# A mixture-of-experts transformer block and a two-layer hybrid block in one kernel: the router by token halves, the branch around the overflow rounds ahead of the last expert sum, the rotary step without TensorE

## Chip, cores and metric

The kernel runs on one core of a Trainium2 chip, in one launch. The metric is the device time of that launch in microseconds (us). PE is TensorE (matrix products; PEld is its weight load), DVE is VectorE, ACT is ScalarE, POOL is GpSimd, and SP is the engine whose queue issues most of the DMAs.

## The reference, cut to what matters

256 tokens of width 1024 go through a first block (three mixers, a layer norm, a mixture of experts, a layer norm) and then through two layers of a second block. Of the first block the part that the change touches is the routing:

```
g_logits = x @ w_rg + b_rg                    # 4 groups
grp = argmax(g_logits);  p_grp = softmax(g_logits)[grp]
e_logits = (x @ w_re[g] + b_re[g]) for g = grp   # 8 experts of that group
top_val, top_idx = top_k(e_logits, 2)
gate = softmax(top_val) * p_grp
out[token] = sum over its 2 experts of gate * ((silu(x @ w_gate[e]) * (x @ w_up[e])) @ w_down[e])
x = layer_norm(ALPHA * x + out)
```

Of the second block:

```
proj = rms_norm(x) @ w_in                 # 24 tiles of 128 columns
dq, dk = apply_rope(...), gq, gk = apply_axial_rope(rms_norm(...))   # x1*cos - x2*sin, x2*cos + x1*sin
three kinds of attention (differential, grouped, memory), each gated by silu
x = x + rms_norm(concat @ w_out)
```

## The kernel before, in words

Everything is float32. Large products are made of three products of float32r halves: `product` (L851 to L853) multiplies high by high, low by high and high by low. ACT makes the high part of each weight tile (`high`, L1572), DVE subtracts it for the low part (`low`, L2187), each about three tiles ahead of PE. `AT_EXPERTS` are the first three tiles of the second block, whose halves are made at the end of the experts.

A list of turns, `TURNS`, fixes the order. Each turn holds jobs and possibly an attention step. A job is one product of PE into bank 6 or 7 in turn, and one copy out of it ("take") by ACT or DVE (`TAKEN_BY_DVE`); job j may start when job j - 2 has been taken. All engines walk through the same list.

The router comes behind the last output product `y1`. DVE normalises the tokens 0 to 127, then 128 to 255 (`moments`, `centred`, `scaled`; ACT makes the inverse root in `layer_stats`). Then four jobs `x1t` turn x (16 transposes), `logit` makes the 36 logits for all 256 tokens, with the 36 router columns as weights, `logitT` turns them back to token order, `route` on DVE picks the group, the two experts and their gates in a chain in which each operation waits for the one before (`link`), and `rank` counts with five products of PE how many earlier tokens chose the same expert.

The 32 experts are worked on in eight bunches of four, each expert with 32 places for tokens. Per bunch DVE writes a matrix of places (`places`) and its product with the gates, PE gathers the tokens through the first (`gather_half`, twice), makes gate and up products (`gate_up`, L1247), turns the hidden values, makes the down products (`down`, L1261) and adds them back through the weighed places (`add_back`, L1233) into four banks of PSUM that collect the sum for all tokens. Overflow rounds for experts with more than 32 tokens stand in a branch on every engine behind the last sum; for these inputs it is not entered. Four products with zeros close the sum (L1352). Expert weights stream in through 21 slots in the order of use. `load_expert` lets SP wait until a slot is free: for the first items of bunch 0 that is `gu_half`, the end of the first half of its gate and up products.

In each layer of the second block ten tiles get the rotary step. PE multiplies the tile by a permutation (`swap`, L1031), so that each row gets its partner 16 rows away, DVE multiplies this with the sines (L1879), the tile with the cosines (L1880), and adds (L1883). Six of the ten stand in the opening of a layer, one behind each of the tiles 1 to 5 and the last after the first scores; the four others (tiles 12 to 15, with a norm factor of `hsq`) in the attention steps.

## Time and profile before

| | us |
|---|---|
| median of 3 runs (lowest, highest) | 754.43 (753.81, 759.05) |
| the profiled execution | 761.98 |
| its span, first to last instruction | 760.2 |
| busy in the span: PE, DVE, ACT, POOL | 682.1, 368.4, 324.3, 16.8 |

The mean granted clock of PE is 0.952 of full speed. Shares of busy time are means over stages that have different limits; the chain that ended last tells which engine was waited for, and windows and the timeline tell it for one stage.

### The profile page before, as it was taken

What the parts mean: (1) busy time and instruction counts of PE and PEld (TensorE: products, weight loads), DVE (VectorE), ACT (ScalarE), POOL (GpSimd) and SP (SyncE); (2) the same over time, 40 slices, a digit from 0 to 9 for tenths busy, and PEclk for the clock granted to TensorE, in tenths of its full rate; (3) what the DMA queues carried; (4) which work ended last, traced back from release to release, by engine and by line L of the source; (5) the groups of instructions that cost most, each with busy time, mean ns of one, the idle gap of its engine ahead of it and who ended that gap; (6) DMA issues with size and microseconds to landing.
All of it is one profiled execution on the core that took longest, in us unless ns stands there. A gap on an engine that the chain in (4) does not pass through costs nothing.

```text
span 760.2 us, 11653 instructions
## 1 busy us (share of the span) xinstructions
PE 682.1 (90%) x4580; PEld 520.5 (68%) x4582; DVE 368.4 (48%) x813; ACT 324.3 (43%) x759; POOL 16.8 (2%) x31
## 2 busy tenths in 40 slices
PE   6989999996599999798796799999979999999986
PEld 4968998695343455264251388878859898888876
DVE  1633657445432132021121456678775466787733
ACT  2565665421000112020120243678865545788742
POOL 5001000000000000000000000000000000000000
PEclk9999999898589999898989899999999999999999
DMA  9967331399959999999999729008163080073301
GB/s 280 340 201 246 111 112 56 123 302 367 315 223 350 414 410 414 415 409 416 414 410 411 251 88 300 1 1 274 61 221 111 1 274 5 1 231 103 111 1 56
DMA packets 94616, 167.80 MB, mean 221 GB/s; under 512 B 4238, under 2 KB 75648, under 8 KB 90464
## 3 DMA queue, kind: packets, MB, share of 16 engines
q1 hardware_dynamic: 92272, 160.88, 59.0%
q0 software_dynamic: 2160, 6.07, 2.3%
q8 instruction: 39, 0.64, 0.3%
q14 instruction: 17, 0.14, 0.1%
q10 hardware_dynamic: 128, 0.08, 0.0%
HBM read 165.93 MB, written 1.07 MB: 220 GB/s over the span
## 4 chain that ended last, share of the span: by engine, by line
PE 72%; SPq 11%; DMA 5%; ACT 5%; DVE 4%; issue 2%; ACTq 0%; DVEq 0%
PE psum L851 13%; PE psum L853 11%; PE psum L852 11%; SPq L741 9%; PE psum L1206 4%; PE psum L1247 4%; PE psum L894 4%; PE psum L1145 3%; DMA ring<-in_w_expert_down_dram 3%; PE psum L1261 3%; PE psum L1192 2%; DMA ring<-in_w_expert_up_dram 2%; PE psum L986 2%; PE psum L1104 2%; PE psum L1233 1%
## 5 line engine op out<-in xcount | busy, mean ns | idle before, releaser
L851 PE MATMUL psum<-a_high,w_high 128*128 128x256 f32 x512 | 150.9, 295 | 2.1 <-ACT q_c L1472 1.3
L853 PE MATMUL psum<-a_high,w_low 128*128 128x256 f32 x512 | 144.7, 283 | 0.0
L852 PE MATMUL psum<-x_low,w_high 128*128 128x256 f32 x512 | 144.6, 283 | 0.0
L2187 DVE TENSOR_TENSOR w_low<-ring,w_high 128x1024 fp32r<-128x1024 f32 (+1 forms) x79 | 111.2, 1421 | 23.4 <-ACT w_high L1572 23.3
L851 PEld LDWEIGHTS psum<-a_high,w_high 128*128 128x128 f32 x512 | 97.7, 191 | 13.8 <-issue 4.7
L1572 ACT ACTIVATE w_high<-ring 128x1024 fp32r<-128x1024 f32 (+1 forms) x79 | 95.9, 1219 | 9.6 <-DMA ring<-in_w_in_dram 6.2
L852 PEld LDWEIGHTS psum<-x_low,w_high 128*128 128x128 f32 x512 | 97.8, 191 | 0.4
L853 PEld LDWEIGHTS psum<-a_high,w_low 128*128 128x128 f32 x512 | 97.8, 191 | 0.0
L851 PE MATMUL psum<-w_high,a_high 128*128 128x256 f32 x240 | 69.6, 290 | 0.0
L852 PE MATMUL psum<-w_low,a_high 128*128 128x256 f32 x240 | 68.5, 285 | 0.0
L1247 PE MATMUL psum<-ring,q_c 128*32 128x512 f32 x320 | 55.1, 682 | 11.0 <-DMA ring<-in_w_expert_up_dram 7.0
L1206 PEld LDWEIGHTS psum<-tiles,x_nat 128*128 128x128 f32 x256 | 55.2, 307 | 9.1 <-issue 9.1
L1206 PE MATMUL psum<-tiles,x_nat 128*128 128x128 f32 x256 | 56.9, 382 | 2.1 <-DVE tiles L2104 2.1
L853 PE MATMUL psum<-w_high,mix_low 128*128 128x256 f32 x192 | 54.8, 286 | 0.0
L2115 DVE TENSOR_SCALAR tiles<-tiles 128x256 f32<-128x256 f32 x8 | 2.3, 292 | 101.2 <-ACT tiles L1620 101.2
L851 PEld LDWEIGHTS psum<-w_high,a_high 128*128 128x128 f32 x240 | 46.7, 195 | 3.2 <-issue 2.3
L852 PEld LDWEIGHTS psum<-w_low,a_high 128*128 128x128 f32 x240 | 46.8, 195 | 0.0
L1620 ACT ACTIVATE tiles<-psum 128x256 f32<-128x256 f32 x8 | 3.1, 383 | 97.1 <-PE psum L1247 97.1
L1247 PEld LDWEIGHTS psum<-ring,q_c 128*32 128x32 f32 x320 | 13.6, 123 | 42.5 <-issue 42.5
L853 PEld LDWEIGHTS psum<-w_high,mix_low 128*128 128x128 f32 x192 | 37.4, 195 | 0.0
L1614 ACT ACTIVATE q_c<-psum 128x512 f32<-128x512 f32 x16 | 9.6, 597 | 62.7 <-PE psum L1206 62.7
L1145 PE MATMUL psum<-const,probs 128*128 128x128 f32 x200 | 32.2, 283 | 4.5 <-DVE probs L1973 2.4
(334 smaller groups left out, 1190.4 us busy)
## 6 DMA issues: line engine op xcount, KB each, us to landing
ring<-in_w_in_dram SPq DMA_DIRECT2D x36, 1024.0 KB, 8.7
ring<-in_w_expert_down_dram SPq DMA_DIRECT2D x24, 1024.0 KB, 18.0
ring<-in_w_expert_gate_dram SPq DMA_DIRECT2D x40, 512.0 KB, 14.6
ring<-in_w_expert_up_dram SPq DMA_DIRECT2D x40, 512.0 KB, 15.3
ring<-in_w_out_dram SPq DMA_DIRECT2D x12, 1024.0 KB, 5.1
ring<-in_w_mem_kv_dram SPq DMA_DIRECT2D x4, 1024.0 KB, 16.5
k_c<-in_w_expert_gate_dram SPq DMA_DIRECT2D x5, 512.0 KB, 14.9
k_c<-in_w_expert_up_dram SPq DMA_DIRECT2D x5, 512.0 KB, 15.9
```

What stands on the lines that cost most here:

```text
L741: sp.dma_start(to[:, SLOT // 2 * m:SLOT // 2 * m + SLOT // 2].rearrange("p (k n) -> p k n", n=DE), w[:, 4 * half:4 * half + 4, :]).then_in ...
L851: pe.matmul(dst, left[0], right[0], start=first, stop=False)
L852: pe.matmul(dst, left[0], right[1], start=False, stop=False)
L853: return pe.matmul(dst, left[1], right[0], start=False, stop=last)
L894: mm = pe.matmul(dst, src[:, k, P * tt:P * tt + P], w[:, k, a:b], start=(k == 0), stop=(k == KC - 1))
L986: mm = pe.matmul(dst[:, 0:T], w[:, k, P * n:P * n + P], memT[l][:, k, :], start=(k == 0), stop=(k == KC - 1))
L1145: mm = pe.transpose(dst[:, P * c:P * c + P], pr[:, a:a + P], ident)
L1206: mm = pe.matmul(dst[:, P * c:P * c + P], x[:, k, :], places2[:, tt, :], start=(tt == 0), stop=(tt == 1))
L1247: mm = pe.matmul(bank(6)[PLACES * e:PLACES * e + PLACES, :], gathered2[b % 2][:, k, PLACES * e:PLACES * e + PLACES], w, start=(k == 0), st ...
L1261: mm = pe.matmul(bank((7, 5)[half])[PLACES * e:PLACES * e + PLACES, :], hiddenT[:, k, PLACES * e:PLACES * e + PLACES], expert_slot(n)[:, a ...
L1572: act.activation(split_like_raw(n)[0], raw_of(n), ACT.Copy).then_inc(highs, 1)
L2187: dve.tensor_tensor(w_l, raw_of(n), as_f32(w_h), ALU.subtract).then_inc(lows, 1)
```

## The change

- Router: `x1t` and `logit` are made per 128 tokens. The tokens are the weights now and the 36 router columns stream, so the logits come out in token order and `logitT` goes. The search for a first maximum merges comparison and multiplication. The mask of closed groups is added in one step. `rank` signals after three of its five products, the other two go to bank 3. The places of bunch 0 are compared at once (`locate_first`), the gates are made later (`gates_of`), and the first half of the gather waits for the places only.
- Experts: ACT makes the sigmoid of the gate (Exp, Ln, Exp), in place of an addition and a reciprocal of DVE. The branch stands on PE, ACT and DVE ahead of the last copies and the last sum, and the last sum closes the accumulation, so the products with zeros go. Overflow rounds each make the sum of the bunch before them.
- The first three low parts of the second block are made by GpSimd. ACT makes the third high part a little later.
- Rotary step: DVE shuffles the rows (`stream_shuffle`), GpSimd multiplies by the cosines into one of two buffers, and the swap jobs go from PE's list.

```diff
+PARTNER = [(m + 16) % 32 for m in range(32)]
-TAKEN_BY_DVE = ("bias", "xt2", "y1", "logit", "logitT", "rank", "swap")
+TAKEN_BY_DVE = ("bias", "xt2", "y1", "logit", "rank")
...
-    jobs += [("x1t", k) for k in range(4)] + [("logit",), ("logitT",), ("rank",)]
+    for tt in range(2):
+        jobs += [("x1t", tt, 0), ("x1t", tt, 1), ("logit", tt)]
+    jobs += [("rank",)]
...
 @@ GpSimd
+            for n in AT_EXPERTS:
+                pool.wait_ge(highs, n + 1)
+                w_h, w_l = split_like_raw(n)
+                pool.tensor_tensor(w_l, raw_of(n), as_f32(w_h), ALU.subtract).then_inc(lows, 1)
             pool.wait_ge(p_ready, JOB[("mv", 0, 1)] + 1)
             for n in range(LAYERS):
                 pool.dma_start(post_row[:, n, :], ...
+            for n, (l, t) in enumerate(ROPES):
+                pool.wait_ge(p_act, taken(JOB[("tile2", l, t)]))
+                if n >= 2:
+                    pool.wait_ge(roped, n - 1)
+                pool.tensor_tensor(cosined[n % 2], tile3[:, t, :], c_("cos_lin" if t < 6 else "cos_ax"), ALU.mult
+                                   ).then_inc(cosine, 1)
 @@ PE
                 elif kind == "x1t":
-                    pe.wait_ge(ln_done, 2)
-                    mm = turn4(dst, x4, job[1])
+                    tt, half = job[1:]
+                    pe.wait_ge(ln_done, tt + 1)
+                    for c in range(4):
+                        mm = pe.transpose(dst[:, P * c:P * c + P], x4[:, tt, 4 * half + c, :], ident)
                 elif kind == "logit":
-                    from_act(("x1t", 3))
+                    tt = job[1]
                     for k in range(KC):
-                        mm = pe.matmul(dst[0:GROUPS + EXPERTS, 0:T], router[:, k, :], xT3[:, k, :],
+                        if k % 4 == 0:
+                            from_act(("x1t", tt, k // 4))
+                        mm = pe.matmul(dst[:, 0:GROUPS + EXPERTS], xT3[:, k, P * tt:P * tt + P], router[:, k, :],
...
-                elif kind == "swap":
-                    l, n = job[1:]
-                    from_act(("tile2", l, n))
-                    mm = pe.matmul(dst[:, 0:T], swap, tile3[:, n, :], start=True, stop=True)
...
-                pe.wait_ge(p_dve, taken(JOB[("rank",)]))
                 pe.wait_ge(setup, 2)
-                pe.wait_ge(placed, 1)
+                pe.wait_ge(located, 1)
                 gather_half(0, 0)
+                pe.wait_ge(p_dve, taken(JOB[("rank",)]))
...
-                    pe.wait_ge(y0_out, b + 1)
-                    pe.wait_ge(y1_out, b + 1)
-                    add_back(backs[b % 2])
+                    if b + 1 < BUNCHES:
+                        pe.wait_ge(y0_out, b + 1)
+                        pe.wait_ge(y1_out, b + 1)
+                        add_back(backs[b % 2])
                 pe.wait_ge(memT_out, KC // 2)
                 with pe.If(some):
...
-                for b in range(4):
-                    mm = pe.matmul(bank(b), zeros_b[:, 0:P], zeros_b[:, :], start=False, stop=True, skip_group_check=True)
-                    if b % 2 == 1:
-                        mm.then_inc(moe_done, 1)
+                pe.wait_ge(y0_out, BUNCHES)
+                pe.wait_ge(y1_out, BUNCHES)
+                add_back(backs[1], last=True)
 @@ ACT
-            def gate_exp(i):
+            def gate_exp(i, then):
                 act.wait_ge(gu_ready, i + 1)
-                act.activation(gate_e, bank(6)[:, 0:DE], ACT.Exp, scale=-1.0).then_inc(gate_exped, 1)
+                then(act.activation(gate_e, bank(6)[:, 0:DE], ACT.Exp, scale=-1.0))
+                then(act.activation(gate_e, gate_e, ACT.Ln, bias=1.0))
+                act.activation(gate_e, gate_e, ACT.Exp, scale=-1.0).then_inc(gate_exped, 1)
...
+                y_due(BUNCHES - 1)
+                y_half()
                 act.wait_ge(y_ready, 2 * BUNCHES)
-                for n in AT_EXPERTS:
-                    high(n)
+                high(AT_EXPERTS[0])
                 layer_stats(1, 0)
+                high(AT_EXPERTS[1])
...
                     if job == ("mk", 0, 1):
+                        high(AT_EXPERTS[2])
                         layer_stats(1, 1)
 @@ DVE
+            def rope(l, n):
+                tl = tile3[:, n, :]
+                m = rope_nth(l, n)
+                if m > 1:
+                    dve.wait_ge(roped, m - 1)
+                dve.wait_ge(p_act, taken(JOB[("tile2", l, n)]))
+                link(dve.stream_shuffle(rope_a, tl, PARTNER))
+                op = dve.tensor_tensor(rope_a, rope_a, c_("sin_lin" if n < 6 else "sin_ax"), ALU.mult)
+                dve.wait_ge(cosine, m)
+                link(op)
+                op = dve.tensor_tensor(tl, cosined[(m - 1) % 2], rope_a, ALU.add)
+                if n >= 12:
+                    dve.wait_ge(p_act, taken(JOB[("hsq", l, n)]))
+                    link(op)
+                    op = dve.tensor_tensor(tl, tl, sq_tile(n), ALU.mult)
+                op.then_inc(roped, 1)
...
-                link(dve.tensor_tensor(score3, values3, wide(best), ALU.is_equal))
-                link(dve.tensor_tensor(score3, score3, order, ALU.mult))
+                for tt in range(2):
+                    op = dve.scalar_tensor_tensor(score3[:, tt], values3[:, tt], best[:, tt:tt + 1], order,
+                                                  ALU.is_equal, ALU.mult)
+                link(op)
...
+            def locate_first(src):
+                dve.wait_ge(ranked, 1)
+                link(dve.tensor_tensor(rank, src[:, 0:2 * EXPERTS], e_sc, ALU.add))
+                for tt in range(2):
+                    op = located_in(0, None, tt)
+                op.then_inc(located, 1)
...
-                then(dve.tensor_scalar(gate_e, gate_e, 1.0, None, ALU.add))
-                then(dve.reciprocal(gate_e, gate_e))
                 then(dve.tensor_tensor(gate_e, gate_e, bank(6)[:, 0:DE], ALU.mult))
...
             def experts():
-                places(0, None, link)
+                gates_of()
+                dve.wait_ge(located, 1)
+                weigh(0)
...
-                for n in AT_EXPERTS:
-                    low(n)
+                dve.wait_ge(y_ready, 2 * BUNCHES)
+                y_half()
                 dve.wait_ge(moe_done, 1)
```

## Rows read from the trace of the kernel before

**Rows 1.** The page, its part 4: the chain that ended last.

```profile
PE 72%; SPq 11%; DMA 5%; ACT 5%; DVE 4%; issue 2%; ACTq 0%; DVEq 0%
```

**Rows 2.** Windows of 1 us: busy times, then PE's clock, DMA share, GB/s.

```profile
182.00:183.00 1.00, 0.00 (x0) 0.00 (x0) 0.96 (x2) 0.00 (x0) 0.00 (x0) 0.80 1.10 375
196.00:197.00 1.00, 0.00 (x0) 0.00 (x0) 0.90 (x7) 0.21 (x1) 0.00 (x0) 0.63 1.10 346
206.00:207.00 1.00, 1.00 (x6) 1.00 (x6) 0.00 (x0) 0.00 (x0) 0.00 (x0) 0.50 0.58 229
208.00:209.00 1.00, 0.70 (x4) 0.41 (x2) 0.00 (x0) 0.26 (x1) 0.00 (x0) 0.50 0.00 0
216.00:217.00 1.00, 1.00 (x11) 0.92 (x9) 0.00 (x0) 0.02 (x1) 0.16 (x1) 1.00 0.59 131
```

**Rows 3.** Timeline of the router: start, duration, engine, operation, idle before and releaser.

```profile
181.09 0.20 ACT L1548 ACTIVATE small<-small 128x1 f32<-128x1 f32 x1
182.29 1.28 DVE L2011 SCALAR_TENSOR_TENSOR x_nat<-x_nat,small,tiles 128x1024 f32<-128x1024 f32 x1
183.73 3.75 PE L901 MATMUL psum<-const,x_nat 128*128 128x128 f32 x16 [5.01 <-DVE x_nat L2011]
184.85 0.60 ACT L1413 ACTIVATE xT<-psum 128x512 f32<-128x512 f32 x1 [3.56 <-PE psum L901]
188.21 5.91 PE L998 MATMUL psum<-xT,router_w 128*36 128x256 f32 x16 [0.73 <-ACT xT L1413]
195.09 0.23 DVE L1855 COPY probs<-psum 128x72 f32<-128x72 f32 x1 [0.47 <-PE psum L1004]
200.16 0.22 DVE L2049 TENSOR_TENSOR probs<-probs 128x64 f32<-128x64 f32 x1
200.53 0.60 PE L1010 MATMUL psum<-probs,const 128*128 128x32 f32 x2 [5.47 <-DVE probs L2049]
201.37 0.61 PE L1012 MATMUL psum<-probs 128*128 128x32 f32 x2
202.94 0.22 DVE L1864 TENSOR_TENSOR probs<-psum,probs 128x64 f32<-128x64 f32 x1 [0.62 <-PE psum L1014]
203.80 0.48 DVE L2100 TENSOR_TENSOR tiles<-probs,const 128x128 f32<-128x128 f32 x2
204.95 3.75 PE L1206 MATMUL psum<-tiles,x_nat 128*128 128x128 f32 x16 [2.12 <-DVE tiles L2104]
```

**Rows 4.** Timeline of the end of the experts.

```profile
418.45 5.15 PE L1261 MATMUL psum<-ring,tiles 128*32 128x512 f32 x32 [0.95 <-DMA ring<-in_w_expert_down_dram]
423.66 0.69 DVE L2123 COPY values<-psum 128x512 f32<-128x512 f32 x1 [6.73 <-PE psum L1261]
424.50 3.67 PE L1233 MATMUL psum<-values,tiles 128*128 128x512 f32 x8 [0.90 <-DVE values L2123]
431.37 1.07 PE L1352 MATMUL psum<-zeros_b 128*128 128x512 bf16 x3 [3.20 <-issue]
```

**Rows 5.** Timeline of the opening of the second block's first layer.

```profile
455.81 0.39 ACT L1463 ACTIVATE tiles<-psum 128x256 f32<-128x256 f32 x1 [1.54 <-PE psum L853]
458.69 0.38 ACT L1463 ACTIVATE tiles<-psum 128x256 f32<-128x256 f32 x1 [1.55 <-PE psum L853]
459.12 0.19 PEld L851 LDWEIGHTS psum<-a_high,w_high 128*128 128x128 f32 x1 [0.44 <-ACT tiles L1463]
462.29 0.38 ACT L1463 ACTIVATE tiles<-psum 128x256 f32<-128x256 f32 x1 [2.28 <-PE psum L853]
472.91 0.60 PE L1031 MATMUL psum<-tiles,const 128*128 128x256 f32 x2
457.17 1.22 DVE L2187 TENSOR_TENSOR w_low<-ring,w_high 128x1024 fp32r<-128x1024 f32 x1 [1.64 <-ACT w_high L1572]
459.58 0.43 DVE L1880 TENSOR_TENSOR tiles<-tiles,const 128x256 f32<-128x256 f32 x1
```

**Rows 6.** A window of 50 us in the steps: columns as in rows 2, PE first.

```profile
480.00:530.00 50.00, 47.87 (x362) 41.43 (x361) 37.86 (x84) 37.15 (x102) 0.00 (x0) 1.00 0.28 89
```

More of the change, by code:

```diff
@@ L241 @@
 TURNS = schedule()
-JOBS = [job for jobs, _ in TURNS for job in jobs]
+JOBS = [job for jobs, _ in TURNS for job in jobs if job[0] != "swap"]
+ROPES = [job[1:] for jobs, _ in TURNS for job in jobs if job[0] == "swap"]
 JOB = {job: n for n, job in enumerate(JOBS)}
@@ L558, in build @@
         rope_a = q_c[:, 7 * T:8 * T]
+        cosined = [router_w[:, 0:T], c_("places")]
         def sq_tile(n):
@@ L634, in build @@
         act_chain, dve_chain, moe_chain = sem("act_chain"), sem("dve_chain"), sem("moe_chain")
+        more_act_chain = sem("more_act_chain")
         stored = sem("stored")
         def rope_nth(l, n):
-            order = [j[2] for j in JOBS if j[0] == "swap" and j[1] == l]
-            return l * len(order) + order.index(n) + 1
+            return ROPES.index((l, n)) + 1
         def silu_nth(l, n):
@@ L1227, in turn_hidden, with add_back @@
                 mm.then_inc(hT_ready, 1)
-            def add_back(back):
+            def add_back(back, last=False):
                 for tt in range(2):
@@ L1233, in add_back @@
                         mm = pe.matmul(bank(2 * tt + half), back[:, P * tt:P * tt + P],
-                                       y_e[:, 512 * half:512 * half + 512], start=False, stop=False,
+                                       y_e[:, 512 * half:512 * half + 512], start=False, stop=last,
                                        skip_group_check=True)
-                mm.then_inc(summed, 1)
+                    if last:
+                        mm.then_inc(moe_done, 1)
+                if not last:
+                    mm.then_inc(summed, 1)
             def gate_up(b, half):
@@ L1364, in _ @@
                 for job in jobs:
+                    if job[0] == "swap":
+                        continue
                     run(job, j)
@@ L1409, in take @@
                     op = act.activation(vecs[:, :], src[:, 0:41], ACT.Copy)
-                elif kind in ("xt", "x1t"):
+                elif kind == "xt":
                     k = job[1]
-                    to = xT_1 if kind == "xt" else xT3
-                    op = act.activation(to[:, 2 * k:2 * k + 2, :], src.rearrange("p (c t) -> p c t", c=2), ACT.Copy)
+                    op = act.activation(xT_1[:, 2 * k:2 * k + 2, :], src.rearrange("p (c t) -> p c t", c=2), ACT.Copy)
+                elif kind == "x1t":
+                    tt, half = job[1:]
+                    op = act.activation(xT3[:, 4 * half:4 * half + 4, P * tt:P * tt + P],
+                                        src.rearrange("p (c t) -> p c t", c=4), ACT.Copy)
                 elif kind == "cnat":
@@ L1681, in _ @@
                 for job in jobs:
+                    if job[0] == "swap":
+                        continue
                     for n in SPLIT_AT.get(j, ()):
@@ L1712, in _ @@
                         layer_stats(0, job[2])
-                    elif job[0] == "logitT":
+                    elif job == ("logit", 1):
                         act.wait_ge(route_dif, 1)
@@ L2269, in _ @@
                 for job in jobs:
+                    if job[0] == "swap":
+                        rope(*job[1:])
+                        for n in lows_now:
+                            low(n)
+                        lows_now = []
+                        continue
                     if job == ("cnat", 0):
@@ L2285, in _ @@
                         lambda_sums()
+                    if job == ("rank",):
+                        locate_first(bank(6 + j % 2))
                     if BY_DVE[j]:
@@ L2297, in _ @@
                         scaled(0, job[2])
-                    if job == ("logitT",):
-                        route()
+                    if job == ("x1t", 0, 0):
+                        dve.memset(ones, 1.0)
+                    if job == ("logit", 1):
+                        choose()
                     if job[0] == "tile2" and job[2] in GATE_TILES:
```

174 lines of the change are left out of this document (86 added, 88 removed).

## The prediction

> **What bounds the kernel now.** I read the page first, then the chain of waits, then windows of one and fifty microseconds, then the timeline of three places. The chain [rows 1] is PE for 72% and the DMA queue of SP for 11%, nearly all of it with the expert weights. So there are three regimes. Before 178 us and after 444 us PE is the bound: 47.87 us busy in the 50 us of [rows 6]. Between, the expert weights are streamed, and the DMA sets the pace. In front of the stream lies the router, a serial stretch in which all engines wait for one another: DMA still works off what was queued, falls silent at 206.6 us, and moves nothing until 216.4 [rows 2], because every slot is full and the first is given back only when the first half of bunch 0's gate and up products is done. Until then 1 us at the router is 1 us of the whole: the stream is full again afterwards and its end at 418.45, where PE waits for the last down weights [rows 4], moves with its start.
>
> **Part 1, the router (removed: one logit job, its copies, some links of DVE's chain; moved: work of the first 128 tokens ahead).** Before [rows 3]: the second half of the layer norm ends at 183.57 (182.29 + 1.28), 16 transposes take 3.75, eight logit products with 256 columns 5.91, and the logits lie in token order at 195.32 (195.09 + 0.23).
> After the change, with PE at its low clock as before: ACT is free at 181.3 (it serves the second variance first, 181.09 + 0.20), copies the first tokens' two halves by 182.5 (0.60 each), and PE makes their eight logit products from 181.95. They load 128x128 weights and stream 36 columns; the nearest rows are the rank products, 0.42 apart at the low clock (two from 200.53, the third from 201.37), so eight take 3.5 at the low clock. Some of them fall before the clock drops, which was at 182.6 [rows 2]: end about 185. Then four transposes (0.94), a copy (0.60), four more transposes and their copy beside the first four products, and the last four products: 185.9, 186.5, about 188.5, 190.3; DVE's addition 0.25. Logits at 190.5 instead of 195.32: -4.8.
> DVE's choice took 5.06 from there to 200.38 (200.16 + 0.22). The change merges two linked operations in each of three searches and drops one link and the multiplication from the mask: a link costs about 0.25 at 64 columns, an unlinked neighbour 0.1. I count 0.13 + 0.38 + 0.21 + 0.22: -0.95.
> Rank: PE's fifth product had to end before DVE began at 202.94; now three are enough (two products of 0.43 less), and between them and the first gather stand one addition (0.26, a 64-column operation with its link) and the two comparisons (0.48) in place of four small operations, these two, and the two that weigh: the gather's start was 2.01 after 202.94, now it is 0.9. Together -2.0. The gate weights and the weighing (nine links, about 2.3) move behind; they are needed only after the second half of the gather, 10 us later, where PE's first half gather and first products cover them. If that cover were gone they would cost 2.3.
> Sum -7.8, taken as **-8**. Bounds: if the clock stays high through logits and rank, the three PE pieces halve and the gather starts 11.9 earlier (logits at 187.2, rank 1.3 shorter at half price); if ACT's copies and the smaller matmuls gain only half of what I say, 5. I take the low clock, since it fell at 182.6 and again at 196.6 with PE as little used as it will be. Is the 8 passed on? The stream was silent for 9.8 us; 8 of them vanish, the last item queued still lands at 206.6, and the first slot comes free at about 207. So yes, all of it, and a gain over about 10 would begin to meet data that is not there.
>
> **Part 2, the end of the experts (moved: the branch ahead of the last sum; removed: the four closing products).** In [rows 4] the last down product of PE begins its run at 418.45 and DVE copies its half from 423.66 to 424.35; the last sum runs 424.50 to 428.17; then PE issues nothing for 3.20 us, the branch; the closing products take 1.07, to 432.44. After: branch from 423.66 to 426.9, the copies beside it, sum 3.67 to 430.5, and nothing more. The first tokens' sum is complete at 428.7 instead of 431.9, but PE's next product starts at 430.5 instead of 432.4: **-1.9**. The following stretch is PE's (memory keys and values), with DVE's layer norm beside it, which gains 3.2 and so stays ahead. DVE and ACT take the branch too, now ahead of the last copies. Both reach it when the last hidden products are turned, before the down products begin at 418.45, and their copies are wanted by 426.9: with 3.2 for each that fits. If theirs took 4 us longer than PE's they would begin to show. Bounds: -3.2 if the layer norm were what ends last, 0 if branch and copies run one after another.
> The gate's reciprocal (ACT now makes the sigmoid by Ln and Exp) shortens DVE's chain before the hidden products by about 1 us per bunch. Nothing is paid for it: behind the first seven stands a gather, behind the last the down weights' arrival [rows 4].
> Low parts of the next layer's first three tiles: DVE 1.22 each [rows 5], on GpSimd not shown in this trace. GpSimd starts them when ACT's high parts are there, at about 428, and PE wants the first at 450. Even 5 us each would fit. What is queued behind them on GpSimd is the load of the post-norm rows, wanted at the end of the layer. 0, but see the third rival.
>
> **Part 3, the rotary step (removed: 20 PE products; added: 20 DVE shuffles, 20 GpSimd products).** A swap product is two records, 0.60 in its row at 472.91, of which the next product overlaps a little: 0.53. Its price is higher in the opening of a layer [rows 5]: the next tile's weight load at 459.12 waited 0.44 for ACT's copy of the tile before, because with the swap in between the tile needs that one's bank. Copies of tiles come 3.60 apart with a swap (458.69 to 462.29), and 2.88 without (455.81 to 458.69). So 0.72 for four swaps a layer. The other two of the opening I take at 0.53, the four in the steps at 0.45, where PE is 96% busy [rows 6] and ACT's exponentials sometimes end last. 2.88 + 1.06 + 1.8 = 5.7 a layer, **-11.5** for both. Bounds: -14.4 if all cost 0.72; -8 if only the opening returns it and the steps do not, with a little lost to DVE.
> On DVE three operations of 0.43 stay three: shuffle, product, sum. The shuffle is in no row; the nearest is the product of the same size, 0.43; bounds 0.2 and 0.9. GpSimd's product of 128x256 is in no row either; nearest again 0.43 on DVE, bounds 0.4 and 3. It starts at ACT's copy, a tile earlier than DVE's rotary step, so even 2.8 would be hidden behind one tile. DVE waits for it, and the low parts of later tiles are queued behind this wait; they are three tiles ahead of PE. Per tile DVE works 1.22 + 1.3 = 2.5 of the 2.88 that are left: the cover becomes thin.
> The Trainium skill ("SBUF — State Buffer", "Who interferes with whom") speaks against this: a DVE instruction with two SBUF inputs contends with a GpSimd instruction that reads SBUF, and one blocks fully. No run here shows it so far. "GPSIMD Engine Reference", section 3.1, has GpSimd's tensor_tensor at 1.96 times DVE's time; by that its product would take about 0.85 (an estimate from the page and 0.43), and the sum would be the same.
>
> **The sum.** 8 + 1.9 + 11.5 = 21.4. The profiled execution took 761.98 us (span 760.2), so 740.6 of its kind; the median of the runs shown is 754.43, 7.5 below, and I take the same 21.4 off: **733.0**. The parts lie behind one another and do not share an engine's time, so they add.
>
> **Rivals.** (a) The router's gain is larger: clock high, 11.9 instead of 8, and perhaps the first gather at half its 3.75 [rows 3] and a like part of the products behind it: 725 to 729. For: PE's pause is 2.3 us now, from 179.7 to 181.95, instead of 5.3. Against: the clock fell at 196.6 though the logit products had run to 194.1 [rows 3].
> (b) The router's gain does not reach the end, since DMA is what ends last: 741. Against it stand the zeros in [rows 2]. It holds only if transfers that start 8 earlier meet something else busy; nothing is.
> (c) DVE becomes the bound of the openings: if each GpSimd product of some 0.9 blocks DVE, its 2.5 per tile becomes 3.4, 0.5 above 2.88, over ten tiles with some lead; the opening then returns about half, and the steps, with DVE 76% busy, lose some too: 6 of 11.5 lost, 739. By the skill's rule this is what would happen; the kernel's rows only leave it room.
> (d) Slower than before: GpSimd's product is so slow that the first scores of each layer wait for the rotary step. They need the fourth tile's, so four products in sequence against 14.4 us of PE's tiles. Each layer loses 4g - 14.4, and the whole 21.4 is eaten at g = 6.3 us, fifteen times DVE's 0.43; at 7 us it gives 760.
> (e) The branch shows on ACT or DVE and part 2 becomes a loss of some us: 736 to 738.
>
> **Chances.** Forecast (sum within 4 us) 0.50; (a) 0.17; (b) 0.07; (c) 0.15; (d) 0.03; (e) 0.08. Eight in ten: 724 to 743. Within 1% (about what a measurement of this kernel can tell from no change) is 747 to 762: reached if (b) and (c) meet, 0.07; slower is (d), 0.03; faster 0.90.
>
> **What the changed profile would show.** The first gather at about 197 instead of 204.95; DMA's gap at 207 to 208.4 instead of 9.8 us; logits in two groups of eight products. The last down product at about 410.5; then 3.2 us of issue ahead of the last sum, and the first memory product 12 us after the start of the last down products instead of 14. Tile copies 2.88 apart in both openings; no line of swaps. GpSimd products under 1 us, and DVE's low parts still 1.22; if they stretch, (c) is at work. What would make it wrong: a clock that behaves differently in the router, a DVE chain slower than its count of links, and GpSimd.

## The result: a third of the forecast gain

The changed kernel took 751.51 us (median of 8 runs, 744.20 to 752.28), the kernel before, on the same chips, 758.52 (8 runs, 753.81 to 763.87). The ratio is 0.989, 95% interval 0.986 to 0.992: 8.3 us faster by the ratio, 7.0 by the medians, where 21.4 were forecast, and outside the forecast's range. Of the 18.5 us between 733.0 and 751.51, 4.1 are the starting point (three runs of before had their median at 754.43, the eight at 758.52); the other 14.4 are gain that did not come.

The profiled execution of the changed kernel took 747.01 us (span 745.2), 15.0 less than that of before. This pair flatters the change: the one lies 4.5 below the median of its kernel, the other 3.5 above.

**The router after.** Timeline; the first row stands against the first of [rows 3], the second variance.

```profile
178.34 0.20 ACT L1571 ACTIVATE small<-small 128x1 f32<-128x1 f32 x1
179.17 2.22 PE L1020 MATMUL psum<-router_w,xT 128*128 128x36 f32 x16 [2.05 <-ACT xT L1435]
183.07 3.60 PE L1020 MATMUL psum<-router_w,xT 128*128 128x36 f32 x16
186.71 0.19 DVE L1897 TENSOR_TENSOR probs<-psum,small 128x36 f32<-128x36 f32 x1 [5.09 <-PE psum L1020]
191.15 0.22 DVE L2085 TENSOR_TENSOR probs<-probs 128x64 f32<-128x64 f32 x1
193.08 0.23 DVE L2093 TENSOR_TENSOR probs<-psum,probs 128x64 f32<-128x64 f32 x1 [1.48 <-PE psum L1028]
193.34 0.50 DVE L2146 TENSOR_TENSOR tiles<-probs,const 128x128 f32<-128x128 f32 x2
193.99 3.75 PE L1218 MATMUL psum<-tiles,x_nat 128*128 128x128 f32 x16 [0.15 <-DVE tiles L2146]
```

From variance to first gather: 204.95 - 181.09 = 23.86 before, 193.99 - 178.34 = 15.65 after, so -8.2. Its pieces: variance to logits 14.23 before and 8.56 after (-5.7); the choice 5.06 and 4.47 (-0.6); choice to gather 4.57 and 2.62 (-1.95). The two groups of logits show the clock: the same 16 records take 2.22 us where it was full until 180.7, and 3.60 after it fell. The other 2.75 us by which the gather is early (204.95 - 193.99 = 10.96 in all) were there before the router began.

**The end of the experts after**, against [rows 4]; and the DMA queues in the silence, as the stretch in which PE issues nothing is called from here on.

```profile
406.92 6.54 PE L1276 MATMUL psum<-ring,tiles 128*32 128x512 f32 x32 [0.86 <-DMA ring<-in_w_expert_down_dram]
413.52 0.69 DVE L2178 COPY values<-psum 128x512 f32<-128x512 f32 x1 [8.02 <-PE psum L1276]
414.95 2.81 PE L1245 MATMUL psum<-values,tiles 128*128 128x512 f32 x6 [1.50 <-DVE values L2178]
420.92 1.02 PE L1245 MATMUL psum<-values,tiles 128*128 128x512 f32 x2 [3.16 <-issue]
421.78 2.54 PE L1004 MATMUL psum<-bias,ring 128*128 128x256 f32 x11
```

```profile
q1 hardware_dynamic: 567, 0.56, 46.3%
q8 instruction: 1, 0.02, 1.9%
```

From the end of the last down product to the next layer's first product it is 8.32 us (413.46 to 421.78) and was 8.64 (423.60 to 432.24): -0.3 instead of -1.9. The silence stayed, and it was not the branch alone: it now stands in the middle of the last sum, behind the branch by 2.8 us of products. The queue rows (columns: packets, MB, share; window 417.5 to 421.2) show what happens in it: one packet of 16 KB on q8, a queue of kind "instruction". In the kernel before one packet of this queue falls into the silence too, between 428.2 and 428.9, and none between 418.5 and 428.1. The profiles do not name the engine that a queue serves, but there are fourteen silences of 2.0 us or more in the eighteen profiles of this document, and each ends 2.4 to 2.8 us after such a packet started, wherever it stands (here 418.48 and 420.92, before 428.54 and 431.37). So I read it as PE waiting for its own code. It does not need full queues: the queues' share is 0.99 in before's silence and falls to 0.27 in this one. The Trainium skill ("Runtime: NRT & Kernel Launch", "Instruction fetch mechanics") says that code comes in 16 KiB blocks, that crossing into the next is mostly hidden, and that a taken branch to code outside the blocks at hand breaks the fetching ahead. The 16 KB packet agrees with the first and the silence of 3.16 us not with the second; on the third see e6 and e15.

**The layers after.** Timeline: layer norm and GpSimd, then copies of tiles (against [rows 5]); then groups of instructions, with busy us and mean ns.

```profile
423.51 1.23 DVE L2048 SCALAR_TENSOR_TENSOR x_nat<-x_nat,small,tiles 128x1024 f32<-128x1024 f32 x1
426.84 2.35 POOL L848 TENSOR_TENSOR w_low<-ring,w_high 128x1024 fp32r<-128x1024 f32 x1 [4.42 <-ACT w_high L1595]
427.28 2.98 DVE L2048 SCALAR_TENSOR_TENSOR x_nat<-x_nat,small,tiles 128x1024 f32<-128x1024 f32 x1 [1.22 <-ACT small L1571]
452.52 0.39 ACT L1486 ACTIVATE tiles<-psum 128x256 f32<-128x256 f32 x1 [1.55 <-PE psum L871]
455.40 0.39 ACT L1486 ACTIVATE tiles<-psum 128x256 f32<-128x256 f32 x1 [1.46 <-PE psum L871]
```

```profile
L858 POOL TENSOR_TENSOR router_w<-tiles,const 128x256 f32<-128x256 f32 x10 | 9.3, 926 | 149.8 <-ACT tiles L1486 109.7 <-ACT tiles L1481 40.1
L858 POOL TENSOR_TENSOR const<-tiles,const 128x256 f32<-128x256 f32 x10 | 7.9, 787 | 40.7 <-ACT tiles L1481 29.0 <-ACT tiles L1486 11.7
L1916 DVE TENSOR_TENSOR q_c<-q_c,const 128x256 f32<-128x256 f32 x20 | 9.1, 454 | 0.7
L1915 DVE STREAM_SHUFFLE q_c<-tiles 128x256 f32<-128x256 f32 x20 | 9.0, 448 | 0.1
```

Tiles are copied 2.88 us apart, GpSimd's products take 0.93 and 0.79 us, the shuffle 0.45: all three as forecast. GpSimd does hold VectorE up where both read long operands (2.98 instead of 1.23 us: VectorE's scaling begins 0.44 after GpSimd's subtraction and ends 1.07 after it), but in a place with slack. By that, the trace agrees with the rule of the Trainium skill that the forecast cited ("SBUF — State Buffer", "Who interferes with whom"). What the forecast did not see is this: the timeline ahead of the second G step of the second layer (a G step is one of the grouped attention), and two windows with the columns of [rows 2]. Then the same place in the kernel before.

```profile
660.35 0.43 DVE L2269 TENSOR_TENSOR tiles<-tiles,k_c 128x256 f32<-128x256 f32 x1 [0.67 <-ACT k_c L1508]
661.46 0.44 DVE L1915 STREAM_SHUFFLE q_c<-tiles 128x256 f32<-128x256 f32 x1
662.99 0.42 DVE L1923 TENSOR_TENSOR tiles<-tiles,q_c 128x256 f32<-128x256 f32 x1
663.33 2.35 DVE L2251 TENSOR_TENSOR w_low<-ring,w_high 128x1024 fp32r<-128x1024 f32 x2
664.69 0.36 PE L869 MATMUL psum<-a_high,w_high 128*128 128x256 f32 x1 [2.00 <-DVE w_low L2251]
```

```profile
661.00:665.00 4.00, 2.00 (x15) 1.68 (x15) 3.65 (x8) 3.97 (x12) 0.00 (x0) 1.00 0.52 165
665.00:669.00 4.00, 4.00 (x23) 4.00 (x22) 3.83 (x10) 2.56 (x8) 0.00 (x0) 0.57 0.52 165
```

```profile
677.14 0.42 DVE L2205 TENSOR_TENSOR tiles<-tiles,k_c 128x256 f32<-128x256 f32 x1
679.95 1.22 DVE L2187 TENSOR_TENSOR w_low<-ring,w_high 128x1024 fp32r<-128x1024 f32 x1
681.32 0.36 PE L851 MATMUL psum<-a_high,w_high 128*128 128x256 f32 x1 [0.65 <-ACT q_c L1472]
```

PE waits 2.0 us for a low part that VectorE makes behind the gates and behind the rotary sums, and then works at a mean clock of 0.57. The step from one G score to the next took 10.80 us before (675.16 to 685.96) and takes 13.22 here (657.61 to 670.83); in the first layer 10.79 and 11.73. The wait is 2.0 us in both layers; the difference between them is the clock, which fell only behind the second (in e4's profile it fell behind both, and both steps take 13.2).

The order of VectorE's work at this place is that of the kernel before: gates, rotary operations, low parts. But there it had hardly any slack. Counted from the scores, the first low part began at 4.79 us and was ready at about 6.0, and the product that needs it ran at 6.16. Now it begins at 5.72, since the first gate waits for ScalarE (it begins at 2.74 instead of 1.98) and the four rotary operations take 0.16 longer, while PE, without the swap product, stands ready at 5.08 instead of 5.51.

### The profile page after: what moved, and what is told of

Read it like the earlier page. It is cut to its first block, busy times and chain, and to the rows that moved or that the text cites. A ratio compares the mean times of both kernels' runs of the same rounds, so it can differ in the third digit from the quotient of the medians.

```text
span 745.2 us, 11661 instructions
## 1 busy us (share of the span) xinstructions
PE 666.1 (89%) x4551; PEld 515.1 (69%) x4552; DVE 351.3 (47%) x810; ACT 330.4 (44%) x775; POOL 41.1 (6%) x54
## 3 DMA queue, kind: packets, MB, share of 16 engines
HBM read 165.95 MB, written 1.07 MB: 224 GB/s over the span
## 4 chain that ended last, share of the span: by engine, by line
PE 60%; SPq 13%; DMA 9%; DVE 8%; ACT 6%; issue 3%; DVEq 0%; ACTq 0%
SPq L746 11%; PE psum L869 11%; PE psum L871 10%; PE psum L870 10%; PE psum L1218 3%; PE psum L1262 3%; DMA ring<-in_w_expert_down_dram 3%; DMA ring<-in_w_in_dram 2%; PE psum L1157 2%; PE psum L1276 2%; DMA ring<-in_w_expert_up_dram 2%; PE psum L912 2%; PE psum L1004 2%; SPq L749 2%; PE psum L1204 2%
## 5 line engine op out<-in xcount | busy, mean ns | idle before, releaser
L2251 DVE TENSOR_TENSOR w_low<-ring,w_high 128x1024 fp32r<-128x1024 f32 (+1 forms) x76 | 107.8, 1430 | 16.1 <-ACT w_high L1595 16.1
L2173 DVE TENSOR_TENSOR tiles<-tiles,psum 128x256 f32<-128x256 f32 x8 | 3.4, 422 | 110.1 <-ACT tiles L1645 110.1
L1245 PE MATMUL psum<-values,tiles 128*128 128x512 f32 x64 | 29.5, 601 | 8.6 <-DVE values L2178 5.5
```

What stands on the lines that cost most here:

```text
L1245: mm = pe.matmul(bank(2 * tt + half), back[:, P * tt:P * tt + P], y_e[:, 512 * half:512 * half + 512], start=False, stop=last, skip_group_ ...
L2251: dve.tensor_tensor(w_l, raw_of(n), as_f32(w_h), ALU.subtract).then_inc(lows, 1)
```

## The experiments

All ratios are to the kernel before on the same chip, with 95% intervals; medians are in us. The changed kernel itself stands at 0.989.

**The parts one by one.** Three kernels make each one part of the change in the kernel before: e1 the router, e2 the rotary step, e3 the end of the experts (sum, branch, sigmoid) with the three low parts on GpSimd. The fourth is the changed kernel with satisfied waits at the head of PE's code:

```
+            for _ in range(40):
+                pe.wait_ge(const_in, 16)
```

> The kernel before with the router's part alone. The forecast's term was 8 us. If the router is worth what the changed profile shows (first gather 8.2 us earlier against the last output product, end of the expert stream 7.4 earlier), this is 8 us below the kernel before, ratio 0.989 to 0.990, and nearly the whole gain of the change. Rival: the two profiles differ by run-to-run luck of PE's clock and the part is worth 4 us or less, ratio 0.995 or above.

> The kernel before with the rotary part alone (no swap products, shuffle on DVE, cosines on GpSimd). The forecast's term was 11.5 us, ratio 0.985. Theory now: only the openings return it (some 3.3 us a layer) and the steps are held by the chain of scores, maximum, exponentials, high part and low part, so that later PE pauses longer and part is given back: 4 to 5 us, ratio 0.994. Rival: nothing at all, the openings' gain is fully given back in the steps, ratio 0.998 to 1.002.

> The kernel before with the end of the experts alone (branch ahead of the last sum, no closing products, sigmoid on ACT, three low parts on GpSimd). The forecast's term was 1.9 us, ratio 0.9975. Theory now: the 3.2 us of silence belong to the fetch of the next block of instructions, not to the branch, and stay on the path wherever a block ends; 0 to 2 us, depending on where this kernel's blocks end. In its profile the silence stands either at the branch or inside the last sum. Rival: the silence is the branch's own cost and stands ahead of the last sum, and the kernel gains 1.9.

> The changed kernel with 40 satisfied waits at the head of PE's program, done while PE waits for the first transfer, so that everything behind lies 40 instructions later in the stream. If the 3.16 us of silence inside the last sum is a fetch at the end of a block of instructions, it moves away from the middle of the sum: either to the branch (then up to 1.5 us are gained) or off the path (3 us). If it belongs to the branch or to a wait, it stays between the third and the fourth product of the last sum, and the time is that of the changed kernel, ratio 0.989.

Measured: e1 753.34, ratio 0.9945 (0.992 to 0.997), 4.2 us faster; e2 753.85, 0.9925 (0.989 to 0.996), 5.7 us; e3 757.88, 1.0003 (0.997 to 1.003), nothing. Their sum, 9.7, agrees with the whole, 8.3, each part being known to 2 or 3 us either way. e4: 748.33, 0.986 (0.982 to 0.991). In e4 the silence has moved, by 40 instructions that do no work, from the seventh record of the sum to the first; with PE's unshifted code it stands at the seventh record in all three profiles that there are (the changed kernel, e5, e14). In e3 it stands ahead of the sum too. The rows are e3's, then e4's:

```profile
427.08 5.37 PE L1237 MATMUL psum<-values,tiles 128*128 128x512 f32 x8 [3.48 <-issue]
```

```profile
415.94 5.37 PE L1248 MATMUL psum<-values,tiles 128*128 128x512 f32 x8 [3.41 <-issue]
```

In both rows the sum also takes 5.37 us instead of 3.67: the clock fell in it (mean 0.67 and 0.68). So a silence there costs 1.7 us more than its own length; e10's, of 3.33 us, did not (3.67 at full clock).

**The pause in the G steps.** e5 and e14 (one kernel, run twice) take the low parts straight after the row maxima:

```
                     maxes(step)
+                    for n in lows_due:
+                        low(n)
...
-                    if not jobs or jobs[0][0] != "swap":
-                        for n in lows_now:
-                            low(n)
```

> The changed kernel with one edit: in every attention step VectorE takes the low part of the next weight slice straight after the step's row maxima, ahead of the gates and ahead of the rotary sums, which the change had put first. Theory (the pause of TensorE at the second G step, 2.2 us in the second layer and some 0.9 us in the first, is VectorE's low part coming late behind the moved rotary work): both pauses shrink to the 0.6 us that the kernel before shows, and the drop of the clock behind the second one goes too; 2.5 to 4 us faster than the changed kernel, ratio to the kernel before 0.984 to 0.986. Rival (the chain scores, row maxima, exponentials, turned product sets these steps, and the rotary sums are now what is late): no gain, 0.989, or a loss of 1 to 2 us.

> The kernel of the low parts taken early, once more. Theory of the layout: 0.982 to 0.986 again, with a silence of about 3 us or two of them between the last down product and the next layer. Rival (luck): 0.976 to 0.980, as the padded ones.

Measured: 745.76, 0.984 (0.980 to 0.989), and 746.70, 0.984 (0.981 to 0.988). In e5's profile the pause is gone in both layers (G step 10.59 us twice), and the clock behind it stays up:

```profile
660.23 2.35 DVE L2251 TENSOR_TENSOR w_low<-ring,w_high 128x1024 fp32r<-128x1024 f32 x2
662.50 0.75 DVE L2269 TENSOR_TENSOR tiles<-tiles,k_c 128x256 f32<-128x256 f32 x2
663.18 0.43 DVE L1915 STREAM_SHUFFLE q_c<-tiles 128x256 f32<-128x256 f32 x1
```

```profile
665.00:669.00 4.00, 4.00 (x34) 3.17 (x34) 3.83 (x11) 3.75 (x11) 0.00 (x0) 1.00 0.50 170
```

Little became late instead (first to last D score, those of the differential attention: 37.37 us, 37.12 in the changed kernel). By ratios and medians, these late low parts cost the changed kernel some 4 to 6 us; each interval by itself meets that of the changed kernel, and the two runs taken together differ from it by a little over two standard errors.

**The branch.** e6 is the changed kernel, e15 that of the low parts, both without the overflow rounds on any engine (these inputs need none, but a kernel without them computes only such inputs).

> The changed kernel without the overflow rounds on every engine: no flag is loaded and no branch is taken at the end of the experts (with these inputs no round is needed, the output is that of the reference). Theory (the silence of 3.2 us at the end of the experts is TensorE's sequencer fetching a block of code that the jump over the rounds kept from being fetched ahead, and the branch itself costs another 0.6 to 0.7 us now that it stands ahead of the last sum): from the last down product to the first product of the next layer 4.6 to 5.2 us instead of 8.3, so 3 to 4 us faster than the changed kernel, ratio 0.984 to 0.985. Rival (a block of code is fetched late there in any layout, because the queues are full of weights): the silence stays at 3.2 us, at another instruction, ratio 0.988 to 0.989.

> Low parts early and no overflow rounds on any engine (none is needed with these inputs). If the two effects are separate they add: 3 us less than without the branch alone, 5 us less than the low parts alone, ratio 0.974 to 0.977, and 4.4 us from the last down product to the next layer. Rival (both had removed the same pause, or their runs were lucky): 0.979 to 0.981.

Measured: e6 743.92, 0.979 (0.974 to 0.984); e15 741.33, 0.976 (0.972 to 0.980). From the last down product to the next layer it is 4.4 us in both, with no silence (of the sixteen profiles with the branch, thirteen have one). The rows are e6's:

```profile
418.43 3.67 PE L1226 MATMUL psum<-values,tiles 128*128 128x512 f32 x8 [0.90 <-DVE values L2142]
421.94 1.24 PE L985 MATMUL psum<-bias,ring 128*128 128x256 f32 x5
```

PE's price of branch and fetch is thus 3.9 us between these two profiles, as expected. The medians gained more, 7.6 against the changed kernel and 5.4 against e14, and e6's ratio lies below the range expected for it; whether the surplus is chance or the branch of another engine was not tried.

**Only the place of the code.** Satisfied waits inside the overflow rounds, which are never entered: 100 of them (e9) and 180 (e10) in the kernel of the low parts, 100 in the changed kernel (e13).

```
                                 more_bunch(n)
+                                for _ in range(100):
+                                    pe.wait_ge(memT_out, KC // 2)
```

> The kernel of the low parts taken early, with 100 satisfied waits added to TensorE's code inside the overflow rounds, which are never entered with these inputs: nothing more is executed, only the code behind the branch lies further on. Theory (the silence is a fetch of code after the jump, and its place is that of a block's border): the 3.2 us move away from the seventh product of the last sum, to another instruction, or vanish where the border falls far enough behind the jump; 0 to 3.3 us faster than the kernel of the low parts alone, ratio 0.980 to 0.984. Rival (the silence belongs to those products, a semaphore or a port): it stays at the same instruction.

> The same with 180 waits in the rounds that aren't entered. Theory: another place again for the silence, and at most one of the two layouts has it before the first product of the sum, where it costs most (3.5 us); a layout without it ends the experts some 3.3 us sooner, ratio 0.980. Rival: as in the run before, no change of place.

> The changed kernel with 100 satisfied waits inside the overflow rounds, which are not entered, and nothing else. Theory (the layout of the code sets how often and where the fetch is exposed): 2 to 4 us faster than the changed kernel, ratio 0.984 to 0.986. Rival (the gain of the padded kernels over the low parts alone was luck of the executions): ratio 0.988 to 0.990.

Measured: e9 742.73, 0.976 (0.972 to 0.980); e10 741.99, 0.9765 (0.973 to 0.980); e13 747.07, 0.984 (0.980 to 0.989). Each median is 3.0 to 4.7 us below those of its kernel without the padding, though nothing more or less is executed. For e9 and e10 the intervals hardly touch those of e5 and e14; e13's meets that of the changed kernel. The profiles show part of it: e9 has almost no silence (PE is idle for 1.73 us ahead of the sum instead of 0.90), e10 has one of 3.33, e13 one of 2.37 and 1.6 us more inside the sum, by the clock (0.68). e14, without padding, has one of 2.20 and e5 two:

```profile
414.24 2.81 PE L1245 MATMUL psum<-values,tiles 128*128 128x512 f32 x6 [3.29 <-issue]
420.20 1.86 PE L1245 MATMUL psum<-values,tiles 128*128 128x512 f32 x2 [3.14 <-issue]
```

From the last down product to the next layer the three profiles without padding (the changed kernel, e5, e14) take 8.7 us in the mean and the four with it (e9, e10, e13, e16) 6.7. With 100 waits the packet of code starts 0.4 to 1.0 us before the last down product ends (e9, e13, e16), in e5 0.5 after it. That is 2.0 of the 3 to 4.7 us; the rest is not explained.

**The same kernels again.** e11 is the kernel before once more, e12 the router part once more, each one execution with its profile (754.93 and 757.57 us).

> The kernel before, once more, for a second profile. Theory (the profile on which the forecast rests shows the clock of the router and of the mixers at its worst): a profile with other stretches of low clock ahead of 215 us and the first gather 2 to 5 us sooner than 204.95. Rival (the low stretches of 141 to 149, 182 to 193 and 196 to 214 us belong to the kernel): the same stretches again, first gather at 204.9.

> The router part alone, once more, for a second profile. Theory: the first gather lies between 194.9 us, as in its first profile, and 198 us, with another pattern of low clock; the mean of its two profiles stands 5 to 8 us ahead of the mean of those of the kernel before. Rival (the pattern belongs to the kernel): first gather again at 194.9 us, and the router's gain at that point again 10 us, so that it is lost further on.

The first four rows are e11's; they answer to the logits and the first gather in [rows 3] and to the last two of [rows 4]. Then its windows.

```profile
185.21 3.62 PE L998 MATMUL psum<-xT,router_w 128*36 128x256 f32 x16 [0.73 <-ACT xT L1413]
199.68 3.75 PE L1206 MATMUL psum<-tiles,x_nat 128*128 128x128 f32 x16 [2.13 <-DVE tiles L2104]
419.21 3.67 PE L1233 MATMUL psum<-values,tiles 128*128 128x512 f32 x8 [0.90 <-DVE values L2123]
422.93 0.81 PE L1352 MATMUL psum<-zeros_b 128*128 128x512 bf16 x3
```

```profile
141.00:149.00 8.00, 7.69 (x46) 5.55 (x47) 4.62 (x14) 4.17 (x9) 0.00 (x0) 1.00 0.56 182
184.00:191.00 7.00, 4.37 (x22) 2.16 (x20) 1.54 (x8) 1.07 (x2) 0.00 (x0) 0.99 1.10 348
```

The windows of the first profile of before, for 141 to 149 and for the logits:

```profile
141.00:149.00 8.00, 7.86 (x28) 5.18 (x26) 4.43 (x13) 2.20 (x7) 0.00 (x0) 0.57 0.51 162
182.00:193.00 11.00, 8.54 (x28) 5.14 (x29) 1.54 (x2) 2.39 (x4) 0.00 (x0) 0.53 1.10 350
```

One kernel, two executions: the first gather at 204.95 and at 199.68, and at the end of the experts a silence of 3.20 us and none at all (here the packet of code came between 416.5 and 417.5, under the down products). What moved the gather is the clock: 27 us low in the router (182 to 193 and 196 to 213) against 20 (181 to 184 and 191 to 208), and 7 us low at 141 to 149 against none there. Only 2.5 of the 5.3 us lie in the router: its second variance stands at 181.09 and at 178.31, so from there to the gather it is 23.86 and 21.37, and the logits, 5.91 and 3.62 us, are nearly all of this difference. e12's gather stands at 197.34, with 24 us low. The means of two, 202.3 and 196.1, put the router's gain there at 6.2 us; by the first pair (204.95 and 194.95) it was 10.0. From variance to gather the router part takes 17.00 (e1) and 16.25 us (e12), so by this length its gain is 6.0.

**Products that keep the clock up.** e7 is the kernel before, e8 the changed one, with products of constants in PE's pauses of the router.

```
+            def fill(n):
+                for _ in range(n):
+                    pe.matmul(bank(3)[:, 0:T], ident, const[:, P:P + T], start=True, stop=True)
```

> The kernel before, with products of constants that nobody reads put into TensorE's pauses in the router stage (11 ahead of the first turned tile, 4 ahead of the logits, 12 ahead of the ranks, 4 ahead of the first gather), so that the clock stays up. Together with the next run it asks how much of the router's forecast gain was the clock of one profiled execution. Theory (the profile of before showed the router at its worst, low for 27 us, and most executions have less of that): the stage ends 4 to 6 us earlier in the profile than that of the kernel before, the median gains only 1 to 3 us, ratio 0.996 to 0.999. Rival (every execution has the low clock there, it is part of the kernel): the median gains what the profile gains, ratio 0.992 to 0.994.

> The changed kernel with the same filling products in the router stage (4 and 2 ahead of the two groups of logits, 10 ahead of the ranks). Theory: the second group of logits takes 2.0 instead of 3.6 us, ranks and turned tiles lose another 1 us; first gather 2 to 3 us earlier, and the whole 1 to 3 us faster than the changed kernel, ratio 0.985 to 0.988. The difference between this run and the one before is the router change without the clock: by the chain of work 4 to 5 us of router, 8.5 to 9.5 us in all. Rival (the stream of expert weights, not the first gather, sets the end of the experts): first gather earlier, the end of the last down product not, ratio 0.989.

Measured: e7 757.66, 0.999 (0.996 to 1.002); e8 747.35, 0.982 (0.976 to 0.987). e7's profile has its first gather 2.5 us earlier and the last down product's end 4.2 earlier than the first profile of before; the ratio of 12 runs is worth less than 1 us. That fits the theory that this first profile was a bad one, but the stage did not end the 4 to 6 us earlier that I expected. e8 is no clean trial: its first fill started only when PE's wait was over and delayed the logits by the 3.4 us that it took (the two groups then ran in 1.98 and 1.87 us, instead of 2.22 and 3.60), the gather came 2.5 us later than in the changed kernel, and still the median is lower. I can't explain that; its interval meets that of the changed kernel.

**GpSimd's three low parts.** e16 is e9 with these three taken back by VectorE.

> The padded kernel of the low parts taken early (ratio 0.976), with the next layer's first three low parts taken back by VectorE as in the kernel before. Forecast on record: 0 us for this part. Theory: within 1 us, 0.975 to 0.978, since the three low parts lie beside the layer norms on either engine. Rival (GpSimd's 2.35 us products hold VectorE up, whose scaling took 2.98 instead of 1.28 us beside one of them): 1.5 to 2 us faster, 0.974, with the last scaling of the layer norm at 1.3 us. Other rival (VectorE's three products of 1.22 us now stand ahead of its layer norm): 2 to 3.5 us slower, 0.979 to 0.981.

Measured: 744.85, 0.980 (0.976 to 0.984), e9 at 0.976 (0.972 to 0.980): not told apart. In its profile the layer norm's last scaling takes 1.28 us instead of 2.10 in e9, but the norm ends 14.1 us after the start of the sum instead of 12.0 (1.7 of it because e16's sum ran at a mean clock of 0.68 and took 5.37 us), and from the first memory product to the first scores it is 36.4 us with either. So the work lies under PE's, wherever it is done.

## Why the prediction was wrong

Right were: the direction; what the edits do in the router and in the openings; GpSimd under 1 us; the tile distance of 2.88; and no rival of the five took the place of the forecast. Wrong were three terms of the sum: in the first a price, in the second what the silence is, in the third a cover taken for granted.

**Part 1, "-8".** The edits return what was worked out: -8.2 between the same two operations of one pair of profiles. The mistake is in what stood under it, one execution of before. The step that failed is the price of the stage before: "eight logit products with 256 columns 5.91" is that of a low clock over most of them, and "PE at its low clock as before" was taken for a property of the kernel. In another execution of the same kernel they take 3.62, and the stage is 2.5 us shorter. So the term of 8 is 6.0 by two profiles each of before and of the part alone, and 4.2 by the ratio of e1, whose interval (2 to 6) just reaches 6.0. How far a run's clock and its time go together can be read from all runs: with the time at low clock in a run taken as 2 x (1 - mean granted clock) x span, 68 runs of before and 116 of the other kernels lie about lines with a slope of 0.25 us for each us at low clock; the runs of before span 45 to 81 us of it and 753 to 765 us of time. As a price of the clock it fails: e7 took 17 us of low clock away and was 0.5 us faster in the mean than before on its chip. "Is the 8 passed on?" was answered rightly: the last down run starts 11.5 us earlier (406.92 against 418.45) where the gather was 11.0 earlier. It then takes 6.54 us instead of 5.15, without a wait inside, at a mean clock of 0.55 instead of 0.70, so 10.1 us are left at its end.

**Part 2, "-1.9".** It came to 0.3 in the profile and to nothing in e3. Failed has the step "then PE issues nothing for 3.20 us, the branch". By all that the runs show it is a wait for code, which moves with the layout of the code, is there in some executions only, and was joined in this profile by 0.6 us ahead of the sum (PE idle for 1.50 us instead of 0.90; in e14, with the same code on PE, it is 0.90). In six profiles with the branch behind the sum the way from down product to next layer is 8.64, 8.70, 8.42, 8.42, 5.27 and 5.27 us (mean 7.5), in the ten with the branch ahead of it 8.32, 8.68, 8.62, 10.90, 8.65, 5.24, 6.84, 7.52, 6.77 and 7.21 (mean 7.9). The closing products' 1.07 us are eaten by this, and by the clock that fell in the sum in five of the ten.

**Part 3, "-11.5".** It was 5.7. The openings pay nearly as forecast, 3.3 us each: from the start of the second memory product to the first scores of the second layer 24.26 before (603.36 to 627.62) and 20.92 after (589.71 to 610.63), 3.94 forecast. "The four in the steps at 0.45" are 1.8 a layer in the sum and 0.8 in the trace (first to last D score: 37.91 before, 37.12 after). And 0.9 and 2.4 us are lost at one G step of each layer, 2.4 where the clock fell behind the wait. The step that failed here is the cover: the forecast saw that "the low parts of later tiles are queued behind this wait" on VectorE and dismissed it with "they are three tiles ahead of PE". At this step the low part was 0.2 us ahead of its product in the kernel before, and it now comes 0.9 us later, 0.8 of it by ScalarE, which the forecast did not look at. 2 x (3.3 + 0.8) - 0.9 - 2.4 = 4.9, against 5.7 by e2's ratio.

**The sum.** "So 740.6 of its kind; ... I take the same 21.4 off" carried the luck of one execution into the gain, and three runs' median into the start.

**What stays open.** Why the block of code is fetched early in one execution and late in another, what more than 2 us the padding gives, why the medians of the kernels without a branch gained more than PE's silence, and why ScalarE comes 0.8 us later in the G step. The best kernels that still hold the overflow rounds are e9 and e10, 0.976 of before, with medians 9 us below that of the changed kernel.

## What to carry to other kernels

A duration from one execution is a price at that execution's clock: before such a row carries a term of a sum, take a second profile, or price the stretch at both levels of the clock. When a job changes its engine or loses its place in a queue, read at every place where it is issued how long what stands behind it was ready before it was needed, not at the usual one: here one low part with 0.2 us of slack cost nearly as much as the whole part returned, and moving a few lines brought it back. A pause marked "issue" near a branch may be code on its way, and the DMA queues of that window tell; then take the branch out or cover it, since moving work around it moves the pause along.

## What the hardware showed

- A block of code that is not there costs PE 2.0 to 3.5 us; it does so in 13 of 18 profiles, in one of them twice. The silence ends 2.4 to 2.8 us after the block's packet started, with the queues full (before) or at a share falling to 0.27 (the changed kernel). Forty satisfied waits at the head of the program moved the place of the stall by six records.
- The same code has another clock in another execution: the stretch of low clock at 141 to 149 us stands whole in six of the 18 profiles, half in three, not at all in nine, and the kernel before is among the first and the last.
- Taking low clock away by products that nobody needs gives little: e7's runs have 17 us less of it than those of before on the same chip (mean 47 against 65) and are 0.5 us faster in the mean.
- VectorE's shuffle of 128x256 takes 0.45 us, as much as an addition; GpSimd's multiplication of this size 0.79 to 0.93 and its 128x1024 subtraction 2.34, where VectorE takes 0.43 and 1.22.
